# A decoder step on one core: a new front, a final norm inside the last FFN block, and new rows and a stacked update in the heads

## What is computed

```
cs = silu(c);  ada = cs @ w_ada + b_ada              # 9 shift/scale/gate vectors of 1024 per sequence
x += 0.5*gate1 * SwiGLU(mod(rmsnorm(x)))             # FFN1, d_ff 2816
h  = mod(rmsnorm(x));  z = h @ w_in                  # gMLP branch, q, k, v, o, gates
mixed = gelu(u) * (tril(W) @ LN(gelu(v)) + b)
heads: chunkwise mLSTM, 4 heads of 256, state C, n, m; prompt starts at C = 0, samples at given states
x += gate2 * ((sig(g_A)*y_A + sig(g_B)*y_B) @ w_out)
x += 0.5*gate3 * SwiGLU(mod(rmsnorm(x)))             # FFN2
y  = mod(rmsnorm(x)) with its own ada vectors        # final norm
```

## Time and profile before

| what | value |
|---|---|
| median of 3 runs (range) | 2975.05 us (2974.89 to 2980.57) |
| the profiled execution's own time | 2982.64 us |
| its span in the trace | 2980.9 us |
| PE busy | 2853.4 us, 96% |
| DVE, ACT, POOL busy | 49%, 29%, 4% |
| mean granted PE clock | 0.976 |

### The profile page before, as it was taken

One profiled execution on the slowest core, in us unless ns is written; L12 is line 12 of the kernel. 1 busy time (PEld: TensorE's weight loads), 2 busy tenths in 40 slices (PEclk: granted clock), 3 DMA queues, 4 the chain that ended last, 5 costly groups with the idle time before them and its releaser, 6 DMA issues. The chain is left out here.

```text
span 2980.9 us, 44355 instructions
## 1 busy us (share of the span) xinstructions
PE 2853.4 (96%) x17489; PEld 2738.9 (92%) x17489; DVE 1445.9 (49%) x3014; ACT 861.9 (29%) x1392; POOL 130.8 (4%) x190
## 2 busy tenths in 40 slices
PE   5899999999999898999999999999899999999997
PEld 3799999999999888989989988998799999999996
DVE  4655454455443736246436434634773434444346
ACT  5422222222213422332333233234531111111114
POOL 2100000000003000000000000000200000000002
PEclk7899999999999999999999999999999999999998
DMA  7133223222210114111111211212111111111111
GB/s 231 45 97 99 98 84 98 98 84 89 66 52 7 57 42 126 50 57 55 53 61 39 66 57 50 69 54 64 54 43 43 42 42 42 42 42 42 42 43 60
DMA packets 167523, 192.98 MB, mean 65 GB/s; under 512 B 7760, under 2 KB 157036, under 8 KB 167349
## 3 DMA queue, kind: packets, MB, share of 16 engines
q1 hardware_dynamic: 166962, 191.12, 20.1%
q10 hardware_dynamic: 342, 0.15, 0.0%
q0 software_dynamic: 96, 0.00, 0.0%
HBM read 172.38 MB, written 18.87 MB: 64 GB/s over the span
## 5 line engine op out<-in xcount | busy, mean ns | idle before, releaser
L521 DVE SCALAR_TENSOR_TENSOR xT<-ps,gate_p,xT 128x384 f32<-128x384 f32 (+1 forms) x624 | 347.3, 571 | 110.5 <-PE ps L801 97.4
L907 PE MATMUL ps<-hhi,mw_hi 128*128 128x384 f32 (+1 forms) x1152 | 387.8, 337 | 9.6 <-DVE mw_lo L1690 7.6
L738 DVE TENSOR_TENSOR hf<-st,ps 128x384 f32<-128x384 f32 x132 | 70.2, 532 | 642.6 <-PE ps L822 640.5
L908 PE MATMUL ps<-hlo,mw_hi 128*128 128x384 f32 (+1 forms) x1152 | 379.4, 329 | 0.0
L909 PE MATMUL ps<-hhi,mw_lo 128*128 128x384 f32 (+1 forms) x1152 | 379.0, 329 | 0.0
L820 PE MATMUL ps<-hhi,wa_hi 128*128 128x384 f32 (+1 forms) x1056 | 349.9, 331 | 16.9 <-DVE wa_lo L728 13.9
L821 PE MATMUL ps<-hlo,wa_hi 128*128 128x384 f32 (+1 forms) x1056 | 347.5, 329 | 0.0
L822 PE MATMUL ps<-hhi,wa_lo 128*128 128x384 f32 (+1 forms) x1056 | 347.1, 329 | 0.0
L820 PE MATMUL ps<-hhi,wb_hi 128*128 128x384 f32 (+1 forms) x1056 | 346.2, 328 | 0.3 <-DVE wb_lo L728 0.3
L822 PE MATMUL ps<-hhi,wb_lo 128*128 128x384 f32 (+1 forms) x1056 | 346.0, 328 | 0.0
L821 PE MATMUL ps<-hlo,wb_hi 128*128 128x384 f32 (+1 forms) x1056 | 345.9, 328 | 0.0
(11 more groups left out here) (295 smaller groups left out, 5141.2 us busy)
## 6 DMA issues: line engine op xcount, KB each, us to landing
ada_raw<-in_w_ada SPq DMA_DIRECT2D x36, 1024.0 KB, 5.1
mw_raw<-in_w_in SPq DMA_DIRECT2D x32, 1024.0 KB, 5.9
wa_raw<-in_w_ffn_in SPq DMA_DIRECT2D x22, 1024.0 KB, 5.1
wb_raw<-in_w_ffn_in SPq DMA_DIRECT2D x22, 1024.0 KB, 5.2
wo_raw<-in_w_ffn_out SPq DMA_DIRECT2D x22, 1024.0 KB, 5.0
ada_raw<-in_w_ada_final SPq DMA_DIRECT2D x8, 1024.0 KB, 5.4
cs<-in_state_mlstm_C SPq DMA_DIRECT2D x32, 256.0 KB, 2.7
out_C_sample<-cs SPq DMA_DIRECT2D x32, 256.0 KB, 2.2
```

The source lines that it names most:

```text
L521: ins = dve.scalar_tensor_tensor(out=xT[:, m, t0:t0 + wp], in0=ps[:, bank, 0:wp], scalar=gate_p[:, m:m + 1], in1=xT[:, m, t0:t0 + wp], op0 ...
L738: dve.tensor_tensor(M["hf"][:, n, 0:w], M["st"][:, n, 0:w], ps[:, up_bank("b", b, i, n), 0:w], ALU.mult).then_inc(C["hidden"].sem, 1)
L907: pe.matmul(out, wh, xh, start=(j == 0), stop=False)
L908: pe.matmul(out, wh, xl, start=False, stop=False)
```

## The change

Three parts. **Front:** `bring_in` is no block any more but a set of streams (`BringIn`) that FFN1's own block starts with. Eight ada groups are made there, in the order 0, 4, 1, 5, 2, 6, 3, 7 (shift and scale of the same tiles); the first three with plain fp32 products (`NATIVE`), without halves. The squares are taken on ACT from the untransposed x with a running sum; POOL forms 1/rms per token, DVE puts it on diagonals, PE spreads it with the `mean` matrix. `lead_pair` runs the n=0 products of block 0 for both weight tiles k tile by k tile. Block 0 carries four ada groups, so groups 8 to 43 lie in blocks 0 to 8. **Tail:** `final_norm` returns a `Final` that FFN2's block calls. The last block's "out" goes in the order of `order` with four banks; ACT squares and scales each piece (`z`), the pieces are transposed in the other banks, and DVE scales them by 1/rms per token and adds the shift row. The shift rows are made at the start of FFN2: POOL spreads columns, PE multiplies them with the identity, ACT copies the rows (`keep_shift_rows`, four copies of 128x512). **Heads:** the m rows and `a_prev` are stored to DRAM in `gates_and_v` and loaded spread over the partitions (`mb`, `ap_`); the products with `sel` go. stage2's transposes use bank 3. C is not cleared, and chunk 0 has no product with it. The sample update stacks high and low parts of 32 rows: (kh, kh, kl) times (vh, vl, vh) in 96 rows, one f32r matmul for each half; `sequence` b now runs in job b + 1. The core of the diff:

```diff
+        FIRST_ADA = 8
+        NATIVE = 3
...
+                def load(self, sp, load_up):
+                    for u in range(3):
+                        for tt in range(3 * u, 3 * u + (3 if u < 2 else 2)):
+                            sp.dma_start(xtok[:, tt, :], I["x_prompt"][0, 128 * tt:128 * tt + 128, :]).then_inc(x_in[u].sem, 16)
+                    sp.dma_start(xtok[0:64, 8, :], I["x_sample"].rearrange("b t d -> (b t) d")).then_inc(x_in[2].sem, 16)
+                    for j, g in enumerate(ORDER):
+                        if j == 5:
+                            load_up("a", 0)
+                            load_up("b", 0)
+                        sp.dma_start(first_raw[j][:, :, :], wa_d[:, :, g * 256:g * 256 + 256]).then_inc(first_in[j].sem, 16)
...
+                    def square(tt):
+                        rows = slice(0, 64 if tt == 8 else P)
+                        if tt >= 2:
+                            act.wait_ge(squared.sem, tt - 1)
+                        act.activation(junk[rows, tt % 2, :], xtok[rows, tt, :], ACT.Square, accum_out=sums[rows, tt:tt + 1]).then_inc(squared.sem, 1)
...
+                    self.copy_rows(act, 0)
+                    for n, (t0, w) in enumerate(UNITS):
+                        act.wait_ge(*mean_done(n + 1))
+                        act.activation(rr[:, t0:t0 + w], ps[:, n, 0:w], ACT.Copy).then_inc(rms_done.sem, 1)
+                    self.high(act, 3)
+                    self.copy_rows(act, 1)
+                    self.high(act, 4)
...
+                    pool.wait_ge(squared.sem, NTT)
+                    pool.tensor_scalar(var[:, :], sums[:, :], 1.0 / D, EPS, ALU.mult, ALU.add).then_inc(made.sem, 1)
+                    pool.wait_ge(*made(7))
+                    pool.tensor_tensor(rr_t[:, :], var[:, :], power[:, :], ALU.pow).then_inc(made.sem, 1)
...
+                    dve.wait_ge(*made(8))
+                    for t in range(NTT):
+                        dve.tensor_scalar(diag[:, t, :], ident[:, :], rr_t[:, t:t + 1], float(D), ALU.mult, ALU.mult).then_inc(diag_made.sem, 1)
+                    self.keep(dve, 0)
+                    self.low(dve, 3)
+                    self.keep(dve, 1)
+                    dve.wait_ge(*rms_done(3))
+
+                    def pair(i):
+                        norm.factors(dve, i)
+                        norm.turn(dve, 2 * i)
+                        norm.turn(dve, 2 * i + 1)
+
+                    def lows(i):
+                        norm.low(dve, 2 * i)
+                        norm.low(dve, 2 * i + 1)
+
+                    pair(0)
+                    self.low(dve, 4)
+                    lows(0)
+                    self.keep(dve, 2)
+                    self.keep(dve, 3)
+                    pair(1)
+                    split("a", 0, 0)
+                    split("a", 1, 0)
+                    lows(1)
+                    split("b", 0, 0)
+                    split("b", 1, 0)
+                    self.low(dve, 5)
+                    self.keep(dve, 4)
+                    self.low(dve, 6)
+                    self.low(dve, 7)
+                    self.keep(dve, 5)
+                    pair(2)
+                    lows(2)
+                    self.keep(dve, 6)
+                    self.keep(dve, 7)
+                    pair(3)
...
+                    pe.wait_ge(*v_kept(4))
+                    self.product(pe, 0)
+                    for g in (21, 23):
+                        pe.wait_ge(*x_wait(g))
+                    for t in range(NTT):
+                        rows = 64 if t == 8 else P
+                        pe.wait_ge(*diag_made(t + 2))
+                        ins = pe.matmul(ps[:, t // 3, 128 * (t % 3):128 * (t % 3) + rows], mean[0:rows, :], diag[0:rows, t, 0:rows],
+                                        start=True, stop=True)
+                        if t % 3 == 2:
+                            ins.then_inc(mean_done.sem, 1)
+                    for j in range(1, 5):
+                        self.product(pe, j)
+                        self.turn(pe, j - 1)
+                    up_pair(0)
+                    self.turn(pe, 4)
+                    self.product(pe, 5)
+                    up_pair(1)
+                    self.turn(pe, 5)
+                    self.product(pe, 6)
+                    self.product(pe, 7)
+                    self.turn(pe, 6)
+                    up_pair(2)
+                    self.turn(pe, 7)
+                    up_pair(3)
...
+                    def lead_pair(p):
+                        for k in (2 * p, 2 * p + 1):
+                            pe.wait_ge(*lo_done(k + 1))
+                            for nm in ("a", "b"):
+                                for i in range(2):
+                                    if k == 0:
+                                        pe.wait_ge(*C[nm + "_lo"](i + 1))
+                                    ins = product(nm, i, 0, k, FIRST_BANKS[i, 0][0 if nm == "a" else 1])
+                                    if k == KT - 1:
+                                        ins.then_inc(C[nm + "_unit"].sem, 1)
+
+                    def lead_up():
+                        ada_product(pe, group(0, 0))
+                        for i, n in FIRST_ORDER[2:]:
+                            q = FIRST_ORDER.index((i, n)) - 2
+                            up("a", i, n, 0)
+                            up("b", i, n, 0)
+                            ada_turn(pe, group(0, q))
+                            if q < 3:
+                                ada_product(pe, group(0, q + 1))
...
+                order = [(2 * p + i, n) for p in range(KT // 2) for n in (0, 2) for i in range(2)] + [(m, 1) for m in range(KT)]
+                def columns(self, pool):
+                    pool.tensor_copy(col[:, :, :], ada[:, ADA_T:ADA_T + KT, 0:1].broadcast_to([P, KT, P])).then_inc(col_made.sem, 1)
+                    for i in range(2):
+                        pool.tensor_copy(col_s[:, :, i, :, :], bc(ada[:, ADA_T:ADA_T + KT, 1:9], 3, STOK)).then_inc(col_made.sem, 1)
+
+                def shift_rows(self, pe):
+                    pe.wait_ge(*col_made(3))
+                    for b in range(4):
+                        for f in range(4):
+                            k = 4 * (b % 2) + f
+                            src = col[:, k, :] if b < 2 else col_s[:, k, :, :, :].rearrange("p a s t -> p (a s t)")
+                            ins = pe.matmul(ps[:, 4 + b, 128 * f:128 * f + 128], src, ident[:, :], start=True, stop=True)
+                        ins.then_inc(shift_mm.sem, 1)
...
+                def turn(self, pe, i, x_added):
+                    c, t, hf = HALVES[i]
+                    if i == 0:
+                        pe.wait_ge(*scaled(16))
+                        pe.wait_ge(*samples_scaled(1))
+                    if i == 12:
+                        pe.wait_ge(*scaled(24))
+                    if i >= 15:
+                        pe.wait_ge(*x_added(21 + i - 15))
+                    elif i >= 3:
+                        pe.wait_ge(*kept(i - 2))
+                    a = start(t)
+                    for f in range(4):
+                        ins = pe.transpose(ps[:, bank(i), 128 * f:128 * f + 128], z[:, 4 * hf + f, a:a + P], ident[:, :])
+                    ins.then_inc(turned.sem, 1)
...
+                    dve.scalar_tensor_tensor(out=dst, in0=ps[r, bank(i), :], scalar=rr_t[r, c:c + 1],
+                                             in1=(shift_s if t == 8 else shift)[r, f], op0=ALU.mult, op1=ALU.add
+                                             ).then_inc(kept.sem, 1)
...
+                            if final:
+                                final.load_root(act)
                             for u in range(24):
                                 act.wait_ge(*C["x_added"](b * 24 + u + 1))
                                 sq.square(act, u)
-
-                    norm.roots(act)
-                    for j in range(3 * KT):
-                        if j == 4:
-                            split("a", 0, 0)
-                            split("b", 0, 0)
-                        if j == KT:
-                            split("a", 1, 0)
-                            split("b", 1, 0)
-                        norm.high(act, j)
-                    norm.high_samples(act)
+                                if final:
+                                    final.scale(act, u)
+                                if final and u == 17:
+                                    final.roots(act, 0)
+                            if final:
+                                final.roots(act, 1)
...
+                        if final:
+                            final.keep_shift_rows(act)
...
+                            if final and last and u == 19:
+                                final.inverses(dve, 0)
+                            if final and last and u >= 19:
+                                final.keep(dve, 2 * (u - 19))
+                                final.keep(dve, 2 * (u - 19) + 1)
...
```

(75 more changed lines are left out.)

888 lines of the change are left out of this document (543 added, 345 removed).

## The result

| kernel | median, us, of how many runs | lowest to highest | ratio to before, 95% interval |
|---|---|---|---|
| before | 2974.97 of 4 | 2974.28 to 2980.57 | |
| after | 2884.25 of 4 | 2878.97 to 2888.68 | 0.969, 0.9667 to 0.9714 |
| after, measured again beside the last runs | 2882.32 of 5 | 2879.97 to 2885.59 | 0.9683, 0.967 to 0.9697 |

The kernel is 90.7 us faster (94.8 in the second measurement, whose before had 2977.13); the forecast was 77 us, 2898, range 2876 to 2930. The time stands inside the range, 14 us under the forecast and just under the band from 2885 to 2910 that the forecast was given, so the question is which term was too small.

A forecast was written before the change was run, and what follows sets the result against it. TensorE, busy 2853.4 of 2980.9 us, was taken as the bound except in front and tail (about 100 + 39 us). Front 22, heads 43 and tail with FFN2's start 12 sum to 77: 2975 - 77 = 2898 us, range 2876 to 2930.

The forecast's parts named there:

- Front: Start through FFN block 0: n=0 projections done at 74, block 0 ends at 152 against 173.93, 22 us gained.
- rival 1: Front: DVE, ACT and PE wait for each other group by group, block 0 ends near 167; 2917 us, chance 0.22.
- late small loads: Front, within rival 1: PE needs ten small loads after the first x unit while DMA is busy; about 3 us.
- Heads: Four heads, where PE time counts one to one: 4 x (3.5 + 5.3 + 0.9 + 2.2 - 0.3) - 3 = 43 us gained.
- Sample update: Heads: the update's pair of products falls from 1.06 to 0.40 us, eight times 0.66: 5.3 us gained per head.
- Second transposes: Heads: in bank 3 they no longer wait for `inter`, 8.9 us over all: 2.2 us gained per head.
- `kws`: Heads, before job 0: two ACT copies come ahead of `kws`, the a_prev product goes: 0.3 us lost per head.
- The clock: Heads: half clock after the wait for `kws` costs 3 us where it happens; let happen in all four: 3 lost in sum.
- part loads: Heads: 12 added per head on SP; PE reaches stage1 some 8 us after `kws`, so covered; nothing counted.
- Rival 4: Heads: parts come late, DVE's in-order wait delays stage1 of job 0; at 30 us landing 2986 us, chance 0.03.
- Tail and second FFN: Final norm moved into the last FFN block gains 17.4 us, FFN2's start comes 5 later: 12 us gained.
- Rival 2: Whole kernel: everything overlaps, few `lead_up` stalls, no drain at 96 rows, no clock fall; 97 us gained, 2878, chance 0.13.

The follow-up runs named there:

- the last runs: After with four edits together (`kws` sooner, shift rows later, ada turns earlier, tail's first sums one unit later): 2869.75 us; beside it after unedited: 2882.32 us.
- run 8: After, with the turns of ada groups 4 and 7 moved ahead of the products of pairs 0 and 2 in PE's order: 2882.36 us.
- runs 5 and 6: The first of the two: after, with the stacked sample update on 128 rows instead of 96: 2890.20 us. The other is run 6.
- run 6: After, with the heads' second transposes put back in bank 4, waiting for `inter` again: 2899.33 us.
- run 1: After, with the sample update again as two fp32 products of 64 rows, part loads of v left out: 2906.71 us.
- run 4: After, with 18 small dummy loads ahead of the six k part loads, meant to issue them 11 us later: 2934.34 us.
- run 10: After, with DVE making the first v and k parts instead of ACT, and waiting for part loads only ahead of its copy of C: 2875.81 us.
- run 7: After, with ACT keeping the shift rows after the second FFN's first eight `norm.high` instead of ahead of them: 2884.04 us in one run.
- run 2: After, with four fp32 products of 257 columns and two of 64 rows added to job 0 of each head, results unused: 2891.66 us.

## Why the forecast held, and where it was short

**Front: right, out of two errors.** Forecast: first pair product near 50, n=0 done at 74, block 0's end 152. Measured 46.55, 77.9 and 151.81. The waits of DVE up to 82 us show where the pairs' 3.9 us went: 17.5 us for seven of PE's turns, some 16 of them behind 29 us, where I took 10 for all of its waits from there on. DVE's own work was some 3 us less than the 31 that I had.

```profile
DVE ada L529 <- PE ps L614: 17.5, 7, 4.8
```

The last pair product and the first product of `lead_up`:

```profile
77.52 0.34 PE L1119 MATMUL ps<-hhi,wb_lo 128*128 128x384 f32 x1
80.60 0.29 PE L247 MATMUL ps<-ada_hi,cs_r 128*18 128x256 f32 x1 [2.74 <-DVE ada_lo L240]
```

Against that stands the other error: stalls and half clock in `lead_up` were 10 us instead of 14 (151.8 - 77.9 - 64), 6.1 of them the two waits for `ada_lo`. The ladder of rival 1 is there (run 8), but at 3.4 to 4.8 us, not 15. The late small loads are there too: PE waited 0 to 2.2 us for them, differently in each execution. The Trainium skill's rule that all queues share the same 16 engines (Trainium Kernel Development and Optimization, Key Constraints) was cited with an estimate of 3; the waits stay under it. Their effect may go beyond it: in runs 5 and 6, which waited longest (2.0 and 2.2), the clock fell too (0.83 and 0.66 from 14 to 24 us, 1.00 in after), and the first pair product came at 49.9 and 50.0, 2.4 us or more behind the other profiles.

**Heads: the step that failed**, 43 forecast, 53.9 without falls and 61.1 in the first pair of profiles.
- m rows 14.0: 14.2. Chunk 0's product 3.6: 3.5. These steps were right to 0.2 us.
- Sample update 21.2: 25.4 (run 1) to 25.8. Two sizes: the pair takes 0.34, not 0.40, and the product behind the 64-row form loses 0.10 that I had not counted. The Trainium skill's rule (TensorEngine Tiling (Array Packing), Tiling Modes) was set against it: a change of mode drains the engine, 96 is no mode, so 26. The runs agree with the rule, in that 96 and 128 rows do not differ (334 ns each) and 64 lose time (1.30 us against 1.04 with 128, run 1). That its sum comes so near is in part luck: it had the pair at 0.24 and nothing behind it, and the two miss by 0.10 each way.
- Second transposes: 8.8 forecast, 10.0 when they are put back (run 6) and 11.9 between the profiles, 11.3 of it waiting and 0.6 the transposes' own. I had priced the wait by the list, which shows 8.9 of the 11.3.
- `kws`: -1.2 forecast, -2.0 measured: the wait grew by 3.3 us over four heads, and the a_prev products that went gave 1.3. Between the marks, which leave out the first of the four, it is -1.5.
- The clock: -3 forecast, because I took it for a property of job 0. It cost 9.6 us in the first profile of before, 3.1 in the first of after and nothing in the second of either: +6.5 in one pair, 0 in the other. The price of a fall in before (3) was right; that it would happen in all four heads was not, since the first profile showed one execution of several.
- The part loads "covered, barely at the upper end": right, with 0.7 us to spare (run 4). The bound of 8 us after `kws` was 9. Rival 4 was the right mechanism at a distance: DVE's wait for the parts stands in the trace, 5.35 us long, and each us beyond the cover costs more than one. The prediction had named such a wait of DVE for a DMA as a sign of being wrong; it came and cost nothing, as PE needs C only 0.7 us after it is made.

In the pair of profiles without falls the distances between PE's starts add up to what the heads gave: 14.2 + 3.5 + 25.8 + 11.9 - 1.5 = 53.9.

**Tail and second FFN: right, in part by luck.** 12 forecast, 12.5 and 14.9 measured. The last block's down products take 34.8 us against 24.0, so 10.8 ahead of the last product's end (9.3 forecast); from there to the end 11.1 (12.3). But the 10.8 hold 3.1 of half clock, which the sum had no term for: in run 10, without it, the down products take 31.6, and the terms that I named come to 7.7. The second FFN's first product comes 3.3 later (2.4 in the second pair of profiles, 5 forecast), for the reason given: run 7 moves the copies and has it back.

The difference between 77 and 94.7 is thus: clock 9.5, update 4.6, second transposes 3.1, and half a us here and there. Rival 2, everything overlaps, came nearest in time (2878) and for a part of its reason, the update without a drain.

What stays open: what makes the clock fall in one execution's heads and not in another's, and whether after is less exposed to it. Its falls are shorter (1.57 against 3.19 each), but run 2, which put the small products back, had none and so can't tell.

## What to carry to other kernels

Measure a changed operand shape with the instruction behind it: part of the loss shows up there, and the cost of a pair alone was 0.10 us short, 32 times. Price a wait by the distance of two starts where there is one to compare with: the list of waits showed 8.9 us where 11.3 were lost. An in-order engine that waits for small loads delays everything behind that wait, so put the wait at the first true use; here moving it and two copies was worth 3 us, and 11 us more of delay cost 12.5 per head. Where one profile shows clock falls in some repetitions of a loop only, profile the same kernel again before a term is made of them.

## What the runs showed of the hardware that was not expected

- Two executions of one program differ in their clock at the same instruction: 0.50 for 6 us in three heads, or 1.00 throughout. The Trainium skill, TensorE: Matmul & The Clock Gate, Part 1, says that the gate's watch runs freely and doesn't restart with the kernel; that fits, and no run here shows the watch itself.
- A 64-row fp32 product delays the first full-row product behind it: 0.25 us to the next instead of 0.15. Four 128-row fp32 passes of the same length and the large product behind them lose nothing (1.04 us against 1.30).
- A 96-row f32r product takes the time of a 128-row one, 334 ns each.
- Small loads on SP's queue go out 0.61 us apart (six in 3.7 us), whether they move 32 KB or, as the dummies of run 4, 1.2 KB: 18 of them made the parts 11.4 us later.
